# RWKV's state over eight chunks: three combined steps on the engines instead of six single ones

## The chip, the cores and the metric

The kernel runs on one core of a Trainium2 chip. Its time is the device time of one execution in microseconds, the median of the runs shown. The core's engines that compute are TensorE (PE; its weight loads are PEld), VectorE (DVE), ScalarE (ACT) and GpSimd (POOL); SyncE (SP) issues transfers. Each engine runs its own instruction stream in order and waits on semaphores for the others.

## The reference

A decoder trunk of two layers on a sequence of 512 positions, width 2048. Per layer one input projection, four mixers (RWKV-7, mLSTM, latent attention, differential attention), a gate, and one output projection:

```python
for l in range(DEPTH):
    h = rms_norm(x, norm_g[l])
    p = h @ w_in[l]
    z, p_rw, p_ml, p_mla, p_da = _split(p, IN_WIDTHS)
    y = concat([beta[0]*rwkv7(p_rw), beta[1]*mlstm(p_ml), beta[2]*mla(p_mla), beta[3]*diff_attn(p_da)])
    x = x + (y * silu(z)) @ w_out[l]
```

The change is in RWKV's recurrence, 8 heads of 64 x 64 state:

```python
def step(S, inp):
    r_t, w_t, k_t, v_t, kk_t, a_t = inp
    sa = einsum('bhvk,bhk->bhv', S, -kk_t)
    S = S * w_t[:, :, None, :] + sa[..., None] * (kk_t * a_t)[:, :, None, :] + v_t[..., None] * k_t[:, :, None, :]
    return S, einsum('bhvk,bhk->bhv', S, r_t)
```

Both kernels cut the 512 positions into `NCH` = 8 chunks of 64. Within a chunk everything is matrix products; between chunks the state obeys S[c+1] = G[c] S[c] + H[c], where G[c] is a 64 x 64 factor and H[c] a 64 x 64 term of the chunk alone.

## The kernel before, in words

**The projection fills everything.** The input projection is 16 groups of columns (`PIECES`, in the order in which the mixers need them), each of 16 steps (one 128-row slice of the weights) of 4 tiles. A tile is three matmuls of 128 x 512 (high x high, low x high, high x low part of the split float32 operands; L793 in `project`). A tile is named (step, tile) below; step n belongs to group n // 16, and tile m of every group accumulates in bank m of the four PSUM banks `ps_proj`. TensorE's program is one stream: the small products of a mixer, and between them `fill(name, head, j)`, which issues the next few tiles of the projection. How many tiles each name gets is the table `FILL` (L100 to 109); `planned` (L238) deals the list of tiles out to the names in program order. Names like `to_z_da` take all tiles up to the end of a group.

**What ScalarE does for the projection.** ScalarE walks the same plan. Where a fill holds the last step of a group (step 16g + 15), ScalarE's `fill` calls `evacuate(g, m)` (L1244): it waits until TensorE has finished that tile, and copies bank m to the staging buffer. ScalarE does nothing else meanwhile, and what stands behind the call in its own program waits with it. TensorE waits for the copy of bank m before it begins tile m of the next group (`s_proj_copied` in `project`):

```python
if k == 0 and g:
    in_bank = g - 1 if m < tiles_of(g - 1) else g - 2
    pe.wait_ge(s_proj_copied, tiles_before(in_bank) + m + 1)
```

So between the last tile m of a group and the first tile m of the next there are three other tiles, and the copy has to be through in that time.

**RWKV.** Two heads go together (a head pair, `hp` 0 to 3; head 0 in partitions 0 to 63 and head 1 in 64 to 127), four pairs per layer, eight in all. Per pair, in this order: fills `rw_lora` and `rw_factors`, the transposes (L989 to L992), `rw_turned`, the Gram products (L1002), the inversion by levels, then `rw_local`: after the products that give G and H of all chunks (L1098, L1101, L1104, 16 matmuls each), ScalarE copies H to `rw_st` (L1528), VectorE adds G's diagonal to give `rw_gt` (L1935, L1939). Then the state: for chunk 1 to 6, two matmuls (one for each head, L1114), a fill of one tile (`rw_state`), and on VectorE two linked additions (L1948), for which TensorE waits before the next chunk. `rw_state_last` is 0 tiles; L1120 and L1125 follow (the bonus sum, and the products of the states with the queries). A float32 matmul of this size shows as two records of the trace, so L1114's two matmuls are four.

**After RWKV** comes mLSTM, four heads. TensorE's order per head: fill `ml_qk`, wait for VectorE's q and k, the scores (L1154), fill `ml_s`, L1162, fill `ml_h`, L1169, L1171, fills `ml_gate` and `ml_rest`. ScalarE's order per head h around the places that matter:

```python
tanh_z(8 + h, ml_z, ml_e)          # L1273: waits until the stores of y have landed
fill("ml_qk", h)                   # ... exps of ml_w (L1590), fill ml_s, two squares ...
fill("ml_gate", h)
load_ln(); act.wait_ge(s_ml_h_var, h + 1)   # a table load; then Ln, Exp (L1605, L1606)
gate_of_convolution(h + 1)         # L1568
fill("ml_rest", h)
keep_y(8 + h, 4 + h, ml_yo, ml_z, ml_e)     # L1281 cast, waits for DVE L1710, stores (L1283, L1284)
```

With `ml_first=25, ml_qk=(19, 6, 13, 13), ml_s=8, ml_h=3, ml_gate=(0, 0, 9, 0), ml_rest=(22, 15, 6, 12)`. In `keep_y`, VectorE's `low_half` (L1710) waits for ScalarE's cast, and VectorE's L1994, which TensorE's scores wait for, stands behind L1710 in VectorE's program.

Where the plan of before puts the last tiles of the groups behind the first changed fill (the same in both layers): (143, 0..3) in `rw_lora` of pair 2, places 1 to 4 (counted from 0); (159, 0..3) in `rw_local` of pair 2, places 2 and 3, and in its first two `rw_state`; (175, 0..3) in `rw_turned` of pair 3, places 1 to 4 of 5; (191, 0..3) in `ml_first`, places 16 to 19; (207, 0..2) in `ml_qk` of head 1, places 3 to 5 of 6, and (207, 3) in `ml_s` of head 1; (223, 0..3) in `ml_rest` of head 2, places 2 to 5 of 6; (239, 0..3) at the end of `to_z_da`, which has 28 tiles.

Of the kernel before, what the change touches and what calls it, by code (L numbers as in the profile page):

```python
# [24 lines left out]
ACT = mybir.ActivationFunctionType  # L25
AX = mybir.AxisListType.X

P = 128
D, T, DEPTH = 2048, 512, 2
NT = T // P  # L30
# [6 lines left out]
NCH = T // RW_CHUNK  # L37
LEVELS = (2, 4, 8, 16, 32)
MASKED = -1e30
# [51 lines left out]
def tiles_of(g):  # L91
# [13 lines left out]
    rw_pu=(2, 2, 2, 2), rw_local=(4, 4, 4, 4), rw_outer=(1, 1, 1, 1), rw_state=(1, 1, 1, 1), rw_state_last=(0, 0, 0, 0),  # L105
# [132 lines left out]
def planned(counts):  # L238
# [27 lines left out]
    for h in range(4):  # L266
        for name in ("rw_lora", "rw_factors", "rw_turned"):
            place(name, h)
        for name in ("rw_gram", "rw_x"):
            place(name, h)  # L270
        for j in range(len(LEVELS)):
            place("rw_level", h, j)
            if j < len(LEVELS) - 1:
                place("rw_step", h, j)
        for name in ("rw_levels", "rw_pu", "rw_outer", "rw_local"):
            place(name, h)
        for j in range(1, NCH - 1):
            place("rw_state", h, j)
        for name in ("rw_state_last", "rw_carried"):
            place(name, h)  # L280
        if h == 0:
            place("to_z_rw", through=G_Z_RW)
        place("rw_gate", h)
# [40 lines left out]
def build(nc, a, out):  # L324

    with ExitStack() as ctx:
# [105 lines left out]
        rw_wl = rg(NCH)  # L432
# [258 lines left out]
        for layer in range(DEPTH + 1):  # L691
# [10 lines left out]
            with nc.Block() as block:  # L702
# [63 lines left out]
                def _(pe):  # L766
# [61 lines left out]
                    def fill(name, h=0, j=0):  # L828
                        for n, m in plan[name, h, j]:
                            (project if n < STEPS else out_early)(n, m)  # L830
# [143 lines left out]
                    for hp in range(4):  # L974
# [121 lines left out]
                        for i in range(NT):  # L1096
                            for c, q, h, half in quarters:
                                mm(ps[half, c, i * P:i * P + 64], rw_pu[q, 4 * h + i, 0:64], rw_bnT[q, i, half],  # L1098
                                   start=True, stop=True)
                            for c, q, h, half in quarters:  # L1100
                                mm(ps[half, c, i * P + 64:(i + 1) * P], rw_ktT[q, i, half], rw_vT[q, i, half],  # L1101
                                   start=True, stop=False)
                            for c, q, h, half in quarters:
                                last = mm(ps[half, c, i * P + 64:(i + 1) * P], rw_bnT[q, i, half],  # L1104
                                          rw_pu[q, 4 * h + i, 64:P], start=False, stop=True)
# [3 lines left out]
                        for c in range(1, NCH - 1):  # L1109
                            if c > 1:  # L1110
                                pe.wait_ge(s_rw_state_ready, (NCH - 2) * hp + c - 1)
                            for h in range(2):
                                half = slice(64 * h, 64 * h + 64)
                                last = mm(ps[half, h, c * 64:(c + 1) * 64], rw_gt[half, c, :], rw_st[half, c, :],  # L1114
                                          start=True, stop=True)
                            last.then_inc(s_rw_state_mm, 1)
                            fill("rw_state", hp, c)
                        fill("rw_state_last", hp)
                        pe.wait_ge(s_rw_state_ready, (NCH - 2) * (hp + 1))
# [103 lines left out]
                def _(act):  # L1223
# [245 lines left out]
                    for hp in range(4):  # L1469
# [57 lines left out]
                        for q in range(2):  # L1527
                            nc.scalar.activation(rw_st[:, 1 + q:NCH + 1:2, :], ps[:, q, :].rearrange("p (i s c) -> p i s c", i=NT, s=2)[:, :, 1, :], ACT.Copy).then_inc(s_rw_h_copied, 1)  # L1528
                        fill("rw_local", hp)
                        for c in range(1, NCH - 1):  # L1530
                            fill("rw_state", hp, c)
# [147 lines left out]
                def _(dve):  # L1679
# [180 lines left out]
                    for hp in range(4):  # L1860
# [70 lines left out]
                        v.tensor_copy(rw_pu[:, 4:8, :], ps[:, 1, :].rearrange("p (i c) -> p i c", i=NT)).then_inc(s_rw_pu_ready, 1)  # L1931
                        dve.wait_ge(s_rw_local, hp + 1)
# [5 lines left out]
                        for q in range(2):  # L1938
                            ins = v.tensor_tensor(rw_gt[:, q:NCH:2, :], rw_wli[:, q:NCH:2, :], ps[:, q, :].rearrange("p (i s c) -> p i s c", i=NT, s=2)[:, :, 0, :], ADD)  # L1939
                            if q:  # L1940
                                ins.then_inc(s_rw_local_ready, 1)
                            else:
                                link(ins)
                        for c in range(1, NCH - 1):
                            dve.wait_ge(s_rw_state_mm, (NCH - 2) * hp + c)
                            for h in range(2):
                                half = slice(64 * h, 64 * h + 64)
                                ins = v.tensor_tensor(rw_st[half, c + 1, :], rw_st[half, c + 1, :], ps[half, h, c * 64:(c + 1) * 64], ADD)  # L1948
                                if h:
                                    ins.then_inc(s_rw_state_ready, 1)  # L1950
                                else:
                                    link(ins)
# [153 lines left out]
```

## Time and profile before

| | |
|---|---|
| median of 3 runs | 2305.7 us (2302.61 to 2306.72) |
| the profiled execution | 2304.52 us, its span 2302.7 us |
| granted TensorE clock, mean | 0.999 |
| TensorE matmul busy | 2266.4 us, 98% of the span |
| GpSimd busy | 1744.8 us, 76% |
| VectorE, ScalarE busy | 1070.6 us (46%), 662.4 us (29%) |

The span is the time from the first to the last instruction in the profile. Busy of TensorE is the union of its matmuls, which overlap one another, so that one matmul's duration is longer than its share of time: the distance from start to start is what it costs in a row. In a timeline, a line is: start, duration, engine, line, operation, output and inputs, shape, count; in brackets the idle time of the engine ahead of it and what ended it.

### The profile page before, as it was taken

The numbers are of one execution on the slowest core, as the hardware profiler recorded it, in microseconds if no ns is written. First come the engines' busy times: TensorE is split into PE (matmuls) and PEld (weight loads), VectorE is DVE, ScalarE is ACT, GpSimd is POOL, SyncE is SP. The second block draws the span as 40 slices with busy tenths as digits, with TensorE's granted clock in tenths as the row PEclk, the third lists the DMA queues.
The fourth block names the chain that finished last, engine by engine and source line by source line (L and its number), as shares of the span: only waits on it lengthen the run. The fifth ranks groups of instructions, "written<-read, shape, count | busy, mean of one in ns | idle before, by whom it ended". The sixth has DMA issues, their size and how long they took to land. (4 is left out here: it accounts for less than half of the span.)

```text
span 2302.7 us, 38356 instructions
## 1 busy us (share of the span) xinstructions
PE 2266.4 (98%) x16032; PEld 1734.8 (75%) x16032; DVE 1070.6 (46%) x1411; ACT 662.4 (29%) x1193; POOL 1744.8 (76%) x1228
## 2 busy tenths in 40 slices
PE   7999999999999999999999999999999999999999
PEld 5767777777777778777777677767777777787777
DVE  5023327456363772465250232475474647625542
ACT  5222222222221332343341232223132213324421
POOL 3677679678587999988637766886685789998884
PEclk9999999999999999999999999999999999999999
DMA  4622343333234545732536232533332345456334
GB/s 161 192 85 78 103 146 116 91 100 99 84 109 134 160 149 173 254 95 77 149 106 175 82 101 82 165 89 97 93 114 83 95 147 165 138 198 230 89 83 128
DMA packets 165487, 288.64 MB, mean 125 GB/s; under 512 B 28792, under 2 KB 36344, under 8 KB 163776
## 3 DMA queue, kind: packets, MB, share of 16 engines
q1 hardware_dynamic: 125216, 211.60, 31.4%
q10 hardware_dynamic: 40096, 74.57, 9.8%
q8 instruction: 126, 2.06, 0.4%
q14 instruction: 49, 0.40, 0.1%
HBM read 234.43 MB, written 51.68 MB: 124 GB/s over the span
## 5 line engine op out<-in xcount | busy, mean ns | idle before, releaser
L752 POOL TENSOR_SCALAR w_hi<-raw 128x512 fp32r<-128x512 f32 x552 | 905.5, 1640 | 359.0 <-PE ps_proj L793 313.6
L762 POOL TENSOR_TENSOR w_lo<-raw,w_hi 128x512 fp32r<-128x512 f32 (+1 forms) x640 | 844.8, 1321 | 151.7 <-ACT w_hi L1251 96.3
L793 PE MATMUL ps_proj<-h_hi,w_hi 128*128 128x512 f32 (+1 forms) x1760 | 726.4, 413 | 6.2 <-POOL w_lo L762 3.5
L793 PE MATMUL ps_proj<-h_lo,w_hi 128*128 128x512 f32 (+1 forms) x1760 | 688.6, 391 | 0.0
L793 PE MATMUL ps_proj<-h_hi,w_lo 128*128 128x512 f32 x1728 | 675.6, 391 | 0.0
L793 PEld LDWEIGHTS ps_proj<-h_hi,w_hi 128*128 128x128 f32 (+1 forms) x1760 | 329.5, 187 | 107.7 <-issue 26.7
L793 PEld LDWEIGHTS ps_proj<-h_lo,w_hi 128*128 128x128 f32 (+1 forms) x1760 | 329.4, 187 | 73.6 <-DVE h_lo L1773 0.2
L793 PEld LDWEIGHTS ps_proj<-h_hi,w_lo 128*128 128x128 f32 x1728 | 325.7, 188 | 66.1 <-issue 7.7
L808 PE MATMUL ps_proj<-w_hi,h_hi 128*128 128x512 f32 x448 | 181.3, 405 | 0.4 <-POOL w_lo L762 0.4
L808 PE MATMUL ps_proj<-w_lo,h_hi 128*128 128x512 f32 x448 | 174.8, 390 | 0.0
L808 PE MATMUL ps_proj<-w_hi,h_lo 128*128 128x512 f32 x448 | 174.8, 390 | 0.0
L793 PE MATMUL ps_proj<-w_hi,h_hi 128*128 128x512 f32 x256 | 105.1, 411 | 0.0
L808 PEld LDWEIGHTS ps_proj<-w_hi,h_hi 128*128 128x128 f32 x448 | 84.2, 188 | 26.0 <-issue 8.5
L1792 DVE TENSOR_REDUCE arena<-ps 128x1 f32<-128x128 f32 (+3 forms) x96 | 47.1, 491 | 121.4 <-PE ps L1205 63.7
L1244 ACT ACTIVATE stage<-ps_proj 128x512 f32<-128x512 f32 (+1 forms) x118 | 66.5, 601 | 124.8 <-PE ps_proj L793 121.5
L793 PE MATMUL ps_proj<-w_hi,h_lo 128*128 128x512 f32 x256 | 99.9, 390 | 0.0
L793 PE MATMUL ps_proj<-w_lo,h_hi 128*128 128x512 f32 x256 | 99.9, 390 | 0.0
L808 PEld LDWEIGHTS ps_proj<-w_lo,h_hi 128*128 128x128 f32 x448 | 84.2, 188 | 18.1 <-issue 1.9
L808 PEld LDWEIGHTS ps_proj<-w_hi,h_lo 128*128 128x128 f32 x448 | 84.1, 188 | 18.0
L1251 ACT ACTIVATE w_hi<-raw 128x512 fp32r<-128x512 f32 (+1 forms) x88 | 48.9, 561 | 148.1 <-PE ps_proj L793 76.5
L1657 ACT ACTIVATE arena<-ps,arena 128x128 f32<-128x128 f32 (+3 forms) x64 | 38.7, 616 | 109.8 <-DVE arena L1793 109.8
L1718 DVE TENSOR_TENSOR arena<-arena,ps_proj 128x512 f32<-128x512 f32 x48 | 31.2, 680 | 68.1 <-PE ps_proj L808 68.1
(349 smaller groups left out, 2953.6 us busy)
## 6 DMA issues: line engine op xcount, KB each, us to landing
raw<-in_w_in_dram SPq DMA_DIRECT2D x480, 256.0 KB, 2.7
raw<-in_w_out_dram SPq DMA_DIRECT2D x128, 256.0 KB, 3.1
projected<-stage SPq DMA_DIRECT2D x116, 256.0 KB, 2.8
arena<-projected ACTq DMA_DIRECT2D x90, 256.0 KB, 3.1
out_dram<-arena ACTq DMA_DIRECT2D x7, 1024.0 KB, 4.8
gated_hi<-arena ACTq DMA_DIRECT2D x24, 256.0 KB, 2.6
gated_lo<-arena ACTq DMA_DIRECT2D x24, 256.0 KB, 3.2
h_hi<-gated_hi SPq DMA_DIRECT2D x8, 768.0 KB, 5.8
```

The costliest lines, as they stand in the source:

```text
L752: nc.gpsimd.tensor_scalar(hi, src, 1.0, None, ALU.mult).then_inc(s_hi_split, 1)
L762: nc.gpsimd.tensor_tensor(lo, src, hi.bitcast(F32), ALU.subtract).then_inc(s_raw_split, 1)
L793: last = mm(ps_proj[rows, m, :], lhsT, rhs, start=(k == 0 and j == 0), stop=(k == KT - 1 and j == len(products) - 1))
L808: last = mm(bank[:, i, :], lhsT, rhs, start=(first and j == 0), stop=(last_k and j == 2))
L1244: nc.scalar.activation(stage[0:rows, m, :], ps_proj[0:rows, m, :], ACT.Copy).then_inc(s_proj_copied, 1)
L1251: nc.scalar.activation(w_hi[:, at_all % N_SPLIT, 0:width], raw[:, at_all % N_RAW, 0:width], ACT.Copy).then_inc(s_hi_by_act, 1)
L1657: nc.scalar.activation((da_p_first, da_p)[half][:, b, 0:(i + 1) * P], ps[:, b, 0:(i + 1) * P], ACT.Exp, scale=da_rq[:, 4 * half + b:4 * ha ...
L1718: v.tensor_tensor(part, part, bank[:, i, :], ADD).then_inc(s_out_added, 1)
L1792: link(v.tensor_reduce(mx[:, b:b + 1], ps[:, b, 0:(i + 1) * P], AX, MAX))
```

## The change

`STATE_STEPS` = 3 replaces the six steps. In step 0 TensorE forms the products of state for chunks 1, 4 and 6, and beside them products of neighbouring chunks' factors (G3 with G4, transposed and not, and G5 with G6). In step 1, states for chunks 2 and 5 and the pair 5-6, and two longer products of factors. In step 2, four products that all start at state 3 and give states 4 to 7. A step issues 12, 10 and 8 matmuls of 64 x 64 (two of before). VectorE adds the states, in steps 0 and 1 copies the products of factors with the halves exchanged (4 instructions each), and in step 2 does one addition. In the local part, G of chunk 7 (not used) goes, copies of G3 and G5 in the other orientation are formed in its place (4 matmuls for 2), and chunk 7's H is left out (4 matmuls fewer). VectorE gets one small copy and does three additions for two. ScalarE's second copy of H has three tiles for four. In `FILL`, `rw_local` goes from 4 to 5 tiles and `rw_state` from 1 to 2 tiles a step, so a head pair takes 5 + 3 x 2 = 11 tiles there, before 4 + 6 x 1 = 10.

(Common indentation is left out in each part.)

```diff
--- before.py
+++ after.py
@@ -36,6 +36,7 @@
 NCH = T // RW_CHUNK
 LEVELS = (2, 4, 8, 16, 32)
+STATE_STEPS = 3
 MASKED = -1e30
 
 
@@ -102,7 +103,7 @@
 la_probs=(13, 13, 13, 13), la_turned=(3, 3, 3, 3), la_gate=(4, 4, 4, 4),
 rw_first=8, rw_lora=(13, 11, 11, 11), rw_factors=(26, 28, 28, 28), rw_turned=(5, 5, 5, 5),
 rw_gram=(4, 4, 4, 4), rw_x=(2, 2, 2, 2), rw_level=(1, 1, 1, 1), rw_step=(1, 1, 1, 1), rw_levels=(1, 1, 1, 1),
-rw_pu=(2, 2, 2, 2), rw_local=(4, 4, 4, 4), rw_outer=(1, 1, 1, 1), rw_state=(1, 1, 1, 1), rw_state_last=(0, 0, 0, 0),
+rw_pu=(2, 2, 2, 2), rw_local=(5, 5, 5, 5), rw_outer=(1, 1, 1, 1), rw_state=(2, 2, 2, 2), rw_state_last=(0, 0, 0, 0),
 rw_carried=(3, 3, 3, 3), rw_gate=(13, 14, 13, 12),
 ml_first=25, ml_qk=(19, 6, 13, 13), ml_s=(8, 8, 8, 8), ml_h=(3, 3, 3, 3), ml_gate=(0, 0, 9, 0), ml_rest=(22, 15, 6, 12),
 da_first=20, da_sums=(14, 10, 10, 10), da_scores=(7, 7, 7, 7), da_half=(14, 16, 16, 16), da_turned=(3, 3, 3, 3),
@@ -274,7 +275,7 @@
         place("rw_step", h, j)
 for name in ("rw_levels", "rw_pu", "rw_outer", "rw_local"):
     place(name, h)
-for j in range(1, NCH - 1):
+for j in range(STATE_STEPS):
     place("rw_state", h, j)
 for name in ("rw_state_last", "rw_carried"):
     place(name, h)
@@ -1095,28 +1096,48 @@
 fill("rw_outer", hp)
 for i in range(NT):
     for c, q, h, half in quarters:
-        mm(ps[half, c, i * P:i * P + 64], rw_pu[q, 4 * h + i, 0:64], rw_bnT[q, i, half],
-           start=True, stop=True)
-    for c, q, h, half in quarters:
+        if 2 * i + c == NCH - 1:
+            mm(ps[half, 1, 3 * P + 64:4 * P], rw_bnT[q, 1, half], rw_pu[q, 4 * h + 1, 0:64], start=True, stop=True)
+            mm(ps[half, 1, 3 * P:3 * P + 64], rw_bnT[q, 2, half], rw_pu[q, 4 * h + 2, 0:64], start=True, stop=True)
+        else:
+            mm(ps[half, c, i * P:i * P + 64], rw_pu[q, 4 * h + i, 0:64], rw_bnT[q, i, half],
+               start=True, stop=True)
+    used = quarters if i < NT - 1 else quarters[:2]
+    for c, q, h, half in used:
         mm(ps[half, c, i * P + 64:(i + 1) * P], rw_ktT[q, i, half], rw_vT[q, i, half],
            start=True, stop=False)
-    for c, q, h, half in quarters:
+    for c, q, h, half in used:
         last = mm(ps[half, c, i * P + 64:(i + 1) * P], rw_bnT[q, i, half],
                   rw_pu[q, 4 * h + i, 64:P], start=False, stop=True)
 last.then_inc(s_rw_local, 1)
 fill("rw_local", hp)
 pe.wait_ge(s_rw_local_ready, hp + 1)
-for c in range(1, NCH - 1):
-    if c > 1:
-        pe.wait_ge(s_rw_state_ready, (NCH - 2) * hp + c - 1)
-    for h in range(2):
-        half = slice(64 * h, 64 * h + 64)
-        last = mm(ps[half, h, c * 64:(c + 1) * 64], rw_gt[half, c, :], rw_st[half, c, :],
-                  start=True, stop=True)
+three, five = rw_gt[:, 0, :], rw_gt[:, NCH - 1, :]
+g_t = [rw_gt[:, c, :] for c in range(NCH - 1)]
+k_34, k_34_turned, k_56, k_345, k_3456 = (rw_wli[:, j, :] for j in range(5))
+state_products = (
+    ((g_t[1], 1), (g_t[4], 4), (g_t[6], 6)),
+    ((g_t[2], 2), (g_t[5], 5), (k_56, 5)),
+    ((g_t[3], 3), (k_34, 3), (k_345, 3), (k_3456, 3)))
+chunk_products = (
+    ((three, g_t[4]), (g_t[4], three), (five, g_t[6])),
+    ((k_34_turned, g_t[5]), (k_34_turned, k_56)),
+    ())
+for step in range(STATE_STEPS):
+    if step:
+        pe.wait_ge(s_rw_state_ready, STATE_STEPS * hp + step)
+    for j, (factor, c) in enumerate(state_products[step]):
+        for half in halves:
+            last = mm(ps[half, 0, j * 64:(j + 1) * 64], factor[half, :], rw_st[half, c, :],
+                      start=True, stop=True)
+        if j < len(chunk_products[step]):
+            lhsT, rhs = chunk_products[step][j]
+            for q, o in swapped:
+                last = mm(ps[o, 1, j * 64:(j + 1) * 64], lhsT[q, :], rhs[q, :], start=True, stop=True)
     last.then_inc(s_rw_state_mm, 1)
-    fill("rw_state", hp, c)
+    fill("rw_state", hp, step)
 fill("rw_state_last", hp)
-pe.wait_ge(s_rw_state_ready, (NCH - 2) * (hp + 1))
+pe.wait_ge(s_rw_state_ready, STATE_STEPS * (hp + 1))
 mm(ps[:, 0, :], bones, rw_sq, start=True, stop=True).then_inc(s_rw_bonus_sum, 1)
 for c in range(1, NCH):
     fed = slice(256 + c // 2 * 64, 256 + c // 2 * 64 + 64)
@@ -1525,10 +1546,10 @@
 act.wait_ge(s_rw_local, hp + 1)
 
 for q in range(2):
-    nc.scalar.activation(rw_st[:, 1 + q:NCH + 1:2, :], ps[:, q, :].rearrange("p (i s c) -> p i s c", i=NT, s=2)[:, :, 1, :], ACT.Copy).then_inc(s_rw_h_copied, 1)
+    nc.scalar.activation(rw_st[:, 1 + q:NCH:2, :], ps[:, q, :].rearrange("p (i s c) -> p i s c", i=NT, s=2)[:, 0:NT - q, 1, :], ACT.Copy).then_inc(s_rw_h_copied, 1)
 fill("rw_local", hp)
-for c in range(1, NCH - 1):
-    fill("rw_state", hp, c)
+for step in range(STATE_STEPS):
+    fill("rw_state", hp, step)
 fill("rw_state_last", hp)
 act.wait_ge(s_rw_carried, hp + 1)
 nc.scalar.activation(rw_kk.rearrange("p (i c t) -> p c i t", i=NT, c=2), y_parts, ACT.Square).then_inc(s_rw_y_squared, 1)
@@ -1929,27 +1950,30 @@
 v.tensor_tensor(xt, xt, ps[:, 2:4, 0:256], SUB).then_inc(s_rw_xt_stepped, 1)
 dve.wait_ge(s_rw_pu_mm, hp + 1)
 v.tensor_copy(rw_pu[:, 4:8, :], ps[:, 1, :].rearrange("p (i c) -> p i c", i=NT)).then_inc(s_rw_pu_ready, 1)
+link(v.tensor_copy(rw_wl[:, 0:NCH:NCH - 1], rw_wl[:, 3:7:2]))
 dve.wait_ge(s_rw_local, hp + 1)
 chunks_ar = rw_ar[:, :, 1, :].rearrange("p i (c t) -> p c i t", c=2)
 link(v.tensor_tensor(chunks_ar, chunks_ar, ps[:, 2:4, 0:256].rearrange("p c (i t) -> p c i t", i=NT), ADD))
 link(v.tensor_tensor(rw_wli, eye64[:, None, :].to_broadcast([P, NCH, 64]), last_w, MUL))
 
 dve.wait_ge(s_rw_h_copied, 2 * hp + 2)
-for q in range(2):
-    ins = v.tensor_tensor(rw_gt[:, q:NCH:2, :], rw_wli[:, q:NCH:2, :], ps[:, q, :].rearrange("p (i s c) -> p i s c", i=NT, s=2)[:, :, 0, :], ADD)
-    if q:
-        ins.then_inc(s_rw_local_ready, 1)
-    else:
-        link(ins)
-for c in range(1, NCH - 1):
-    dve.wait_ge(s_rw_state_mm, (NCH - 2) * hp + c)
-    for h in range(2):
-        half = slice(64 * h, 64 * h + 64)
-        ins = v.tensor_tensor(rw_st[half, c + 1, :], rw_st[half, c + 1, :], ps[half, h, c * 64:(c + 1) * 64], ADD)
-        if h:
-            ins.then_inc(s_rw_state_ready, 1)
-        else:
-            link(ins)
+link(v.tensor_tensor(rw_gt[:, 2:NCH:2, :], rw_wli[:, 2:NCH:2, :], ps[:, 0, P:].rearrange("p (i s c) -> p i s c", i=NT - 1, s=2)[:, :, 0, :], ADD))
+link(v.tensor_tensor(rw_gt[:, 0, :], rw_wli[:, 0, :], ps[:, 1, 3 * P + 64:4 * P], ADD))
+v.tensor_tensor(rw_gt[:, 1:NCH:2, :], rw_wli[:, 1:NCH:2, :], ps[:, 1, :].rearrange("p (i s c) -> p i s c", i=NT, s=2)[:, :, 0, :], ADD).then_inc(s_rw_local_ready, 1)
+products = ps[:, 0, 0:256].rearrange("p (j c) -> p j c", j=4)
+chunked = ps[:, 1, 0:192].rearrange("p (j c) -> p j c", j=3)
+dve.wait_ge(s_rw_state_mm, STATE_STEPS * hp + 1)
+link(v.tensor_tensor(rw_st[:, 2, :], rw_st[:, 2, :], products[:, 0, :], ADD))
+link(v.tensor_tensor(rw_st[:, 5:8:2, :], rw_st[:, 5:8:2, :], products[:, 1:3, :], ADD))
+link(v.tensor_copy(rw_wli[0:64, 0:3, :], chunked[64:P, :, :]))
+v.tensor_copy(rw_wli[64:P, 0:3, :], chunked[0:64, :, :]).then_inc(s_rw_state_ready, 1)
+dve.wait_ge(s_rw_state_mm, STATE_STEPS * hp + 2)
+link(v.tensor_tensor(rw_st[:, 3, :], rw_st[:, 3, :], products[:, 0, :], ADD))
+link(v.tensor_tensor(rw_st[:, 6:8, :], rw_st[:, 6:8, :], products[:, 1:3, :], ADD))
+link(v.tensor_copy(rw_wli[0:64, 3:5, :], chunked[64:P, 0:2, :]))
+v.tensor_copy(rw_wli[64:P, 3:5, :], chunked[0:64, 0:2, :]).then_inc(s_rw_state_ready, 1)
+dve.wait_ge(s_rw_state_mm, STATE_STEPS * hp + 3)
+v.tensor_tensor(rw_st[:, 4:8, :], rw_st[:, 4:8, :], products, ADD).then_inc(s_rw_state_ready, 1)
 dve.wait_ge(s_rw_bonus_sum, hp + 1)
 link(v.tensor_tensor(rw_bonus, ps[:, 0, :], vv, MUL))
 dve.wait_ge(s_rw_rstd, hp + 1)
```

## Rows read from the trace of the kernel before

**Rows 1.** The page, part 1: busy us (share of the span) and instructions, by engine.

```profile
PE 2266.4 (98%) x16032; PEld 1734.8 (75%) x16032; DVE 1070.6 (46%) x1411; ACT 662.4 (29%) x1193; POOL 1744.8 (76%) x1228
```

**Rows 2.** Timeline of layer 0, TensorE: start us, us, engine, line, operation [idle before].

```profile
230.62 0.47 PE L793 MATMUL ps_proj<-h_hi,w_hi 128*128 128x512 f32 x1 [0.53 <-ACT stage L1244]
```

**Rows 3.** Timeline, first head pair: local products and state, TensorE.

```profile
428.99 0.34 PE L1098 MATMUL ps<-arena 64*64 64x64 f32 x8
...
430.55 0.50 PE L793 MATMUL ps_proj<-h_hi,w_hi 128*128 128x512 f32 x1
...
433.49 0.33 PE L1114 MATMUL ps<-arena 64*64 64x64 f32 x4
...
434.64 0.20 PEld L1114 LDWEIGHTS ps<-arena 64*64 64x64 f32 x4 [0.36 <-DVE arena L1948]
...
440.35 1.02 PE L1120 MATMUL ps<-arena,always 128*128 128x512 f32 x2
```

**Rows 4.** The same stretch, VectorE.

```profile
425.09 0.69 DVE L1931 COPY arena<-ps 128x512 f32<-128x512 f32 x1 [1.27 <-PE ps L1075]
...
432.13 0.88 DVE L1939 TENSOR_TENSOR arena<-arena,ps 128x256 f32<-128x256 f32 x2
...
433.87 0.47 DVE L1948 TENSOR_TENSOR arena<-arena,ps 64x64 f32<-64x64 f32 x2 [0.86 <-PE ps L1114]
```

**Rows 5.** The same stretch, the products of states with queries.

```profile
441.30 0.89 PEld L1125 LDWEIGHTS ps<-arena 64*64 64x64 f32 x28 [0.76 <-issue]
```

**Rows 6.** Timeline, a wait of TensorE that VectorE ends.

```profile
401.95 1.40 DVE L1909 TENSOR_TENSOR arena<-ps,arena 128x512 f32<-128x512 f32 x2
...
403.41 0.27 PE L1020 MATMUL ps<-arena 64*64 64x64 f32 x1 [0.18 <-DVE arena L1909]
```

**Rows 7.** Timeline, layer 0, mLSTM head 0 to head 1, ScalarE, VectorE and TensorE.

```profile
781.56 0.64 ACT L1281 ACTIVATE arena<-arena 128x512 fp32r<-128x512 f32 x1 [2.96 <-DVE arena L1701]
...
785.65 1.09 DVE L1710 TENSOR_TENSOR arena<-arena 128x512 fp32r<-128x512 f32 x1
...
786.67 1.21 DVE L1994 SCALAR_TENSOR_TENSOR arena<-arena 128x1024 f32<-128x1024 f32 x1
786.78 0.33 ACTq L1283 DMA_DIRECT2D gated_hi<-arena  x1
...
789.32 0.39 PE L793 MATMUL ps_proj<-h_hi,w_hi 128*128 128x512 f32 x1
...
790.43 0.58 ACT L1244 ACTIVATE stage<-ps_proj 128x512 f32<-128x512 f32 x1
...
790.68 2.32 PE L1154 MATMUL ps<-arena 128*128 128x512 f32 x8
```

**Rows 8.** Timeline, layer 0, mLSTM head 2, ScalarE and TensorE.

```profile
836.90 1.28 ACT L1287 ACT_TABLE_LOAD   x1
...
840.09 0.64 ACT L1605 ACTIVATE arena<-arena 128x512 f32<-128x512 f32 x1 [1.70 <-DVE arena L2013]
...
842.58 1.04 ACT L1568 ACTIVATE arena<-arena 128x1024 f32<-128x1024 f32 x1
...
845.35 2.64 ACT L1244 ACTIVATE stage<-ps_proj 128x512 f32<-128x512 f32 x4 [1.72 <-PE ps_proj L793]
...
845.83 0.39 PE L793 MATMUL ps_proj<-h_hi,w_hi 128*128 128x512 f32 x1
```

**Rows 9.** Timeline, layer 0, pair 3, behind the transposes.

```profile
669.47 2.07 ACT L1244 ACTIVATE stage<-ps_proj 128x512 f32<-128x512 f32 x4
...
669.81 0.39 PE L793 MATMUL ps_proj<-h_hi,w_hi 128*128 128x512 f32 x1
```

**Rows 10.** Timeline, layer 1, pair 2, `rw_lora`.

```profile
1691.37 0.39 PE L793 MATMUL ps_proj<-h_hi,w_hi 128*128 128x512 f32 x1
...
1691.49 1.58 ACT L1244 ACTIVATE stage<-ps_proj 128x512 f32<-128x512 f32 x3 [0.72 <-PE ps_proj L793]
...
1692.23 0.47 PE L793 MATMUL ps_proj<-w_hi,h_hi 128*128 128x512 f32 x1
```

## The prediction

> **What bounds the kernel now.** The page's first part shows TensorE with a matmul in flight for 98% of the span, the next engine at 76% [rows 1]. So time goes down only by what TensorE stops doing between its matmuls, and it goes up by everything that makes TensorE wait. I then asked for the waits, longest in total first. No wait of TensorE's on VectorE in the six steps is over 0.4 us. One other kind is to be kept in mind: TensorE waits for ScalarE's copy of a finished bank, 0.53 us at one place [rows 2]. Last I read the timelines of the first state stage, and of each place where ScalarE copies banks behind it.
>
> In the state stage the reader is to see a period of 1.15 us from step to step (433.49 to 434.64), six of them 6.86 us in all [rows 3]. A tile of the projection costs 0.68 us (six matmuls in 1.36 us, 789.32 to 790.68 [rows 7]). The other 0.47 us are the four records and the change to the small matmuls and back. The view blames VectorE for 0.36 us, but VectorE was done at 433.87 + 0.47 = 434.34, 0.30 us before TensorE went on [rows 3, 4]; where VectorE really holds TensorE, the gap from its end (403.35) to the matmul is 0.06 us [rows 6]. So VectorE isn't what a step costs; the switch is.
>
> **The change, part by part, for one head pair.**
>
> *Three switches fewer.* The six tiles stay, so 3 x 0.47 = 1.41 us go.
>
> *More small products.* 60 records instead of 24, of which 12 are in the three switches that stay. With all four quadrants of the array in turn, 96 records took 1.56 us (428.99 to 430.55 [rows 3]), 0.016 us each; with two quadrants, 28 took 0.76 us (0.89, less a load's 0.13) from first to last start [rows 5], 0.028 each. Step 0 (24 records in four quadrants) costs 0.38 us, step 1 (16 and 4) 0.37, step 2 (16 in two) 0.45; less 3 x 0.11 for the twelve already counted it is +0.87 us. Net: -0.54 us.
>
> *The local products.* Four matmuls go, two come. But those for G3 and G5 stand two by two on the same quadrant, and their eight records go at the two-quadrant rate, or one after the other. I take +0.25 us; bounds 0 and +0.4 (eight records at 2 x 0.028, none hidden).
>
> *VectorE between steps.* With a gap of 0.03 us behind each, an addition from PSUM takes 0.22 us at 64 columns and 0.42 at 256, and a copy at 512 0.69 [rows 4]: about 0.15 us and 1.05 ns a column. The trace has no copy that crosses the halves on VectorE; I take the same price. Step 0's four instructions are 0.22 + 0.28 + 0.35 + 0.35, with three gaps: 1.29 us. VectorE begins 0.38 us after a step's first matmul at four records (433.49 to 433.87), so some 0.65 at 24, and ends at 1.94; with 0.06 TensorE may go on at 2.00. Its own work lasts 0.38 + 0.36 (the switch) + 2 x 0.68 = 2.10. It is covered, by 0.1 us; from there on each 0.1 us of the two copies costs a pair 0.2. Step 1 is 1.15 us of VectorE, with 0.24 to spare, step 2 0.42: covered. The third addition of G and the small copy ahead of it add 0.3 us; TensorE has one more tile (0.68) to cover that, and VectorE had 0.48 us to spare (432.13 + 0.88 against 433.49 [rows 3, 4]).
>
> So a pair gains 0.54 - 0.25 = 0.29 us, eight pairs 2.3 us. Bounds: 5 us gained, or 1 us lost if the copies are slow.
>
> *The plan moves.* A pair now takes 11 tiles in these fills, before 10. The total is the same (`to_z_da` gives up four), but every later tile comes earlier in program order: by 1 tile after pair 0, and by 4 from mLSTM on. With them move ScalarE's copies of the finished banks, against ScalarE's other work. TensorE must have the copy of tile m three tiles, 2.04 us, after it finished that tile. I go through each end of a group.
>
> (191) lands at places 12 to 15 of `ml_first`, (159) wholly in `rw_local`, (239) is again the end of its fill: ScalarE has nothing between the copies there. Nothing changes.
>
> (207): now tile 0 is the *last* place of `ml_rest` of head 0, tiles 1 to 3 are places 0 to 2 of `ml_qk` of head 1, and (208, 1) is place 4. Between them stand `keep_y` and `tanh_z`. `ml_rest` ends with the matmul that starts 13 before 789.32, 786.37, and ends at 786.76. ScalarE, idle since 778.6, waits for it, copies to 787.4 (0.58), and only then makes the cast that before began at 781.56: 787.35 to 788.0. VectorE's L1710 (before at 785.65) starts at 788.05; the stores are issued 1.13 us behind its start, at 789.2; and from there to ScalarE's next copy of a bank, through the landing of the stores and L1273, before took 790.43 - 786.78 = 3.65 us. So (207, 1) is copied from 792.8 to 793.4. TensorE wants to begin (208, 1) at 789.32. It goes on at about 793.5 (a copy's end to the matmul is 0.16 us in [rows 10]): **4.2 us lost** [rows 7]. L1994, before at 786.67 to 787.9, slips to 790.3, still ahead of the scores. The bounds: 3.8, if L1710 is 0.4 us shorter, and 5.1, if the stores land later.
>
> (223): tiles 0 and 1 are now places 7 and 8 of `ml_gate` of head 2, ahead of `load_ln`; tiles 2 and 3 are places 0 and 1 of `ml_rest`, and (224, 2) is place 4. Before, ScalarE waited 1.72 us for (223, 0) at 845.35; four tiles earlier it is 842.63, and (223, 1) is copied by 843.9. Only now come the table load and its activation (1.5 us, 836.90 and on), then L1605 at 845.4, and L1568 2.49 us behind it (840.09 to 842.58) at 847.9. The copy of (223, 2) follows at 848.9 and ends at 849.5. TensorE wants (224, 2) at 845.83, and begins it at 849.65: **3.8 us lost** [rows 8]. The scores of head 3 are later by the same, which leaves VectorE's chain to them, 5.3 us late, still in time.
>
> (175): tiles 2 and 3 are now places 0 and 1 of `rw_turned`, and (176, 2) is place 4, at 669.81. ScalarE's first copy behind its work on the transposes is 669.47 to 670.06, and it is now that of (175, 2): 0.4 us lost [rows 9].
>
> (143): tile 0 is now in `rw_gate`, 1 to 3 in `rw_lora`, places 0 to 2. In layer 1 ScalarE's first copy there is done at 1692.0, TensorE went on at 1692.23 and would want it at 1691.37: 0.9 us, of which 0.2 were there before [rows 10]. In layer 0, where pair 2 has one activation less, about 0.1.
>
> A word on ScalarE's table loads. The load in head 2's chain is 1.28 us [rows 8]. The Trainium skill, "ScalarE: Activation LUTs", section "Rules for kernel authors", budgets about 2.7 us for every switch to another set. By its price the chain of (223), with two switches in it, would be some 2.8 us longer per layer, and the kernel 5.6 us slower than by the row; the row is for this very load, so I stay with it and give the rule no chance of its own.
>
> **The sum.** Layer 0: 4.2 + 3.8 + 0.4 + 0.1 = 8.5; layer 1: 4.2 + 3.8 + 0.4 + 0.7 = 9.1. Lost 17.6, gained 2.3: +15.3 us. The profiled execution of before took 2304.5 us, 1.2 under the median of the runs shown; it comes to 2319.8, and the median to 2321. Nothing gives the loss back: TensorE is the last engine in every stage behind it.
>
> **The rivals.**
>
> *The copies are hidden; the steps decide.* For it: at (223) ScalarE had 1.72 us to spare, and no wait of this kind is over the 0.53 us of [rows 2] by much. It asks that ScalarE's copy isn't stuck behind `keep_y` and the table load, that is, that my places of the tiles are wrong. Against it: where they were, they explain the rows of before (three copies ahead of L1154 and one behind, four behind L1568). Then only the 2.3 us are gained: 2303. If the local products cost nothing more either, 2301.
>
> *Half of it.* Only one of the two long stalls appears, for instance because ScalarE's cast and L1710 run in another order than I read: 2321 less 2 x 4, 2313.
>
> *VectorE becomes the bound in the steps.* With crossing copies at twice the price a pair loses 0.70 - 0.10 = 0.60 us in step 0 and 0.56 - 0.24 = 0.32 in step 1; it decides from a copy of 0.40 us on, in place of 0.35. Alone, without my stalls: 8 x (0.92 - 0.29) = 5 us slower, 2311. With them 2328. This is the one by which the steps themselves make the kernel slower. Against it: no row shows an operation of VectorE on half the partitions that is dearer than by its columns (L1948).
>
> *The local products cost more than the steps save.* By 0.4 us a pair for the two quadrants instead of 0.25: 1 us more, within the range.
>
> **How the numbers follow.** The stalls as worked out, 0.72: 2321, its own range 2316 to 2326. Half of them 0.10: 2313. Copies hidden 0.13: 2303, of which half at 2301 or below. VectorE as bound 0.05, with or without the stalls. From 2309 to 2327 the time should be found 8 times in 10. A change of less than 0.2% (4.6 us, 2301.1 to 2310.3) can't be told from none: faster 0.06, same 0.10, slower 0.84.
>
> **What would show it.** Each step right: in the timeline of each pair, three groups of L1114's successor 2.1 us apart, and 0.3 to 0.6 us less from the first to the bonus sum. In the waits: TensorE at L793 for ScalarE's L1244, some 17 us in all, in pieces of 4.2 and 3.8 in both layers, in `ml_qk` of head 1 and `ml_rest` of head 2. In ScalarE's lines: L1281 of head 0 five to six us later against TensorE, right behind a copy. I am wrong if that wait stays near 1 us, and the prediction then fails in the places of the tiles; if the pieces are there and smaller, it fails in the chain from cast to landing.

## The result, and the profile after

The changed kernel takes 2323.9 us (median of 4 runs, 2323.4 to 2325.6), the kernel before on the same chip 2304.8 (2302.6 to 2306.7). The ratio is 1.0085, with a 95% interval of [1.0072, 1.0097]: 19 us slower. The forecast was 2321, by its own sum 15.3 us slower.

The profiled execution took 2323.97 us, its span is 2322.2, and the mean granted clock 0.995 (before: span 2302.7, 0.999). Part 1 of the page of the changed kernel, to be laid beside [rows 1]; the second line is the costliest group of its part 5 (busy, mean ns of one | idle before it, what ended most of it):

```profile
PE 2271.0 (98%) x16288; PEld 1742.8 (75%) x16288; DVE 1069.8 (46%) x1403; ACT 662.1 (29%) x1193; POOL 1742.1 (75%) x1228
...
L794 PE MATMUL ps_proj<-h_hi,w_hi 128*128 128x512 f32 (+1 forms) x1760 | 727.1, 413 | 21.2 <-ACT stage L1265 17.6
```

Of the 19.5 us between the two spans TensorE is busy for 4.6; the other 15 us are idle time, and it stands in front of the projection, ended by ScalarE's copies. (The change shifts the lines: L793 is L794 now, L1244 is L1265, L1114 is L1131 and L1136, L1281 is L1302, L1710 is L1731, L1605 is L1626.) The view of waits says so too (total us, how many, the longest). The changed kernel's line, where the kernel before has 2.2 us in 4 waits, the longest 0.6:

```profile
PE ps_proj L794 <- ACT stage L1265: 18.2, 11, 4.2
```

**The first head pair.** Timeline of the changed kernel, TensorE and VectorE (start, us, engine, line, operation, [idle before]), to be laid beside [rows 3, 4]:

```profile
427.69 0.34 PE L1103 MATMUL ps<-arena 64*64 64x64 f32 x8
...
429.23 0.50 PE L794 MATMUL ps_proj<-h_hi,w_hi 128*128 128x512 f32 x1
...
432.86 0.27 PE L1131 MATMUL ps<-arena 64*64 64x64 f32 x2
...
433.37 0.50 PE L794 MATMUL ps_proj<-h_hi,w_hi 128*128 128x512 f32 x1
433.50 0.22 DVE L1966 TENSOR_TENSOR arena<-arena,ps 128x64 f32<-128x64 f32 x1 [1.57 <-PE ps L1136]
...
434.08 0.36 DVE L1968 COPY arena<-ps 64x192 f32<-64x192 f32 x1
...
434.48 0.35 DVE L1969 COPY arena<-ps 64x192 f32<-64x192 f32 x1
...
434.96 0.28 PE L1131 MATMUL ps<-arena 64*64 64x64 f32 x2
...
437.05 0.68 PE L1131 MATMUL ps<-arena 64*64 64x64 f32 x16
...
439.16 1.02 PE L1141 MATMUL ps<-arena,always 128*128 128x512 f32 x2
```

The three steps start at 432.86, 434.96 and 437.05: 2.1 us apart, as forecast. From the first to the bonus sum are 6.30 us, before 6.86 [rows 3]: 0.56 less, 4.5 in eight pairs. The local products, without the state's, take 1.54 us (427.69 to 429.23), before 1.56: they cost nothing more. VectorE's two copies across the halves take 0.36 and 0.35 us; the forecast had 0.35.

**mLSTM, head 0 to head 1**, changed kernel, beside [rows 7]:

```profile
786.42 0.60 ACT L1265 ACTIVATE stage<-ps_proj 128x512 f32<-128x512 f32 x1 [8.21 <-PE ps_proj L794]
...
786.91 0.62 ACT L1302 ACTIVATE arena<-arena 128x512 fp32r<-128x512 f32 x1
...
787.57 1.05 DVE L1731 TENSOR_TENSOR arena<-arena 128x512 fp32r<-128x512 f32 x1 [2.23 <-ACT arena L1302]
...
788.71 0.39 PE L794 MATMUL ps_proj<-h_lo,w_hi 128*128 128x512 f32 x1
...
791.75 0.63 ACT L1294 ACTIVATE arena<-arena 128x512 f32<-128x512 f32 x1 [1.57 <-DMA gated_lo<-arena]
792.28 0.58 ACT L1265 ACTIVATE stage<-ps_proj 128x512 f32<-128x512 f32 x1
...
792.91 0.79 PE L794 MATMUL ps_proj<-h_hi,w_hi 128*128 128x512 f32 x1 [3.81 <-ACT stage L1265]
793.51 0.63 PE L794 MATMUL ps_proj<-h_hi,w_lo 128*128 128x512 f32 x1
...
795.64 3.94 PE L1175 MATMUL ps<-arena 128*128 128x512 f32 x8
```

Before, the cast on ScalarE (L1281) ran at 781.56, when VectorE had its operand ready. Now the copy of tile (207, 0) stands ahead of it, and that copy waits 8.21 us for TensorE. From there all goes in file: copy, cast, L1731, the stores, their landing (1.57 us of waiting), L1294, and only then the next copy of a bank. TensorE meanwhile has run through the four tiles whose banks were free, (207, 1) to (208, 0), and stands still from 789.1 to 792.91. And behind the wait it runs at half its rate: matmuls of 512 columns start 0.42 us apart instead of 0.23, and the eight of the scores take 3.94 us where they took 2.32 [rows 7].

**Head 2**, changed kernel, beside [rows 8]:

```profile
849.23 1.28 ACT L1265 ACTIVATE stage<-ps_proj 128x512 f32<-128x512 f32 x2 [5.74 <-PE ps_proj L794]
...
850.52 1.28 ACT L1308 ACT_TABLE_LOAD   x1
...
852.05 0.63 ACT L1626 ACTIVATE arena<-arena 128x512 f32<-128x512 f32 x1
852.20 0.39 PE L794 MATMUL ps_proj<-h_lo,w_hi 128*128 128x512 f32 x1
852.70 1.28 ACT L1627 ACT_TABLE_LOAD   x1
...
854.53 1.04 ACT L1589 ACTIVATE arena<-arena 128x1024 f32<-128x1024 f32 x1
...
855.48 1.06 ACT L1265 ACTIVATE stage<-ps_proj 128x512 f32<-128x512 f32 x2
856.11 0.50 PE L794 MATMUL ps_proj<-h_hi,w_hi 128*128 128x512 f32 x1 [3.52 <-ACT stage L1265]
```

Again two copies wait 5.74 us for TensorE in front of a table load, two activations and a second load, and the next two copies wait behind them. Layer 1 has the same two waits, of 4.23 and 3.52 us; the small ones are 0.15 us (pair 3, in both layers) and, in layer 1, 0.60 (pair 2).

The granted clock by windows of the changed kernel (window, its length, busy us and instructions by engine, granted clock, DMA share, GB/s): the stretch behind each wait of layer 0, then the whole of mLSTM:

```profile
792.90:799.30 6.40, 6.39 (x13) 4.12 (x14) 0.00 (x0) 2.37 (x6) 1.23 (x1) 0.53 0.94 304
856.90:860.30 3.40, 3.40 (x10) 2.61 (x9) 3.22 (x6) 0.63 (x1) 1.70 (x2) 0.51 0.96 297
...
743.24:931.40 188.16, 180.56 (x755) 141.06 (x754) 101.50 (x119) 51.09 (x80) 161.82 (x109) 0.97 0.49 154
```

The same stage of layer 0 in the kernel before:

```profile
743.63:922.09 178.46, 178.19 (x766) 140.69 (x766) 103.17 (x119) 51.32 (x80) 165.39 (x111) 1.00 0.52 162
```

So behind each long wait the chip grants the lower of TensorE's two levels, 1.2 in place of 2.4 GHz, for some microseconds. The stage is 9.7 us longer in layer 0, though it now holds four tiles less (2.72 us): 12.4 us are lost there, of which the two waits are 7.65 us from start to start (3.97 and 3.68). Most of the rest is the clock, as e4 shows (4.4 us); 0.3 us have no row.

### The profile page after: what moved, and what is told of

Read it like the earlier page. It is cut to its first block and busy times, and to the rows that moved or that the text cites. A ratio compares the mean times of both kernels' runs of the same rounds, so it can differ in the third digit from the quotient of the medians.

```text
span 2322.2 us, 38868 instructions
## 1 busy us (share of the span) xinstructions
PE 2271.0 (98%) x16288; PEld 1742.8 (75%) x16288; DVE 1069.8 (46%) x1403; ACT 662.1 (29%) x1193; POOL 1742.1 (75%) x1228
## 5 line engine op out<-in xcount | busy, mean ns | idle before, releaser
L794 PE MATMUL ps_proj<-h_hi,w_hi 128*128 128x512 f32 (+1 forms) x1760 | 727.1, 413 | 21.2 <-ACT stage L1265 17.6
L794 PE MATMUL ps_proj<-h_lo,w_hi 128*128 128x512 f32 (+1 forms) x1760 | 690.5, 392 | 0.0
L794 PE MATMUL ps_proj<-h_hi,w_lo 128*128 128x512 f32 x1728 | 678.0, 392 | 0.0
L794 PEld LDWEIGHTS ps_proj<-h_hi,w_hi 128*128 128x128 f32 (+1 forms) x1760 | 330.6, 188 | 125.1 <-issue 27.0
L794 PEld LDWEIGHTS ps_proj<-h_lo,w_hi 128*128 128x128 f32 (+1 forms) x1760 | 330.6, 188 | 74.1
L794 PEld LDWEIGHTS ps_proj<-h_hi,w_lo 128*128 128x128 f32 x1728 | 326.9, 189 | 67.3 <-issue 7.7
L1265 ACT ACTIVATE stage<-ps_proj 128x512 f32<-128x512 f32 (+1 forms) x118 | 66.9, 599 | 172.9 <-PE ps_proj L794 168.7
L794 PE MATMUL ps_proj<-w_hi,h_hi 128*128 128x512 f32 x256 | 104.8, 410 | 0.6 <-ACT stage L1265 0.6
L794 PE MATMUL ps_proj<-w_hi,h_lo 128*128 128x512 f32 x256 | 99.9, 390 | 0.0
L794 PE MATMUL ps_proj<-w_lo,h_hi 128*128 128x512 f32 x256 | 99.9, 390 | 0.0
L809 PEld LDWEIGHTS ps_proj<-w_lo,h_hi 128*128 128x128 f32 x448 | 84.2, 188 | 18.2 <-issue 1.9
```

What stands on the lines that cost most here:

```text
L794: last = mm(ps_proj[rows, m, :], lhsT, rhs, start=(k == 0 and j == 0), stop=(k == KT - 1 and j == len(products) - 1))
L809: last = mm(bank[:, i, :], lhsT, rhs, start=(first and j == 0), stop=(last_k and j == 2))
L1265: nc.scalar.activation(stage[0:rows, m, :], ps_proj[0:rows, m, :], ACT.Copy).then_inc(s_proj_copied, 1)
```

## The experiments

**e1: the change with the old plan.** One tile less in `rw_local`, so a pair again takes ten:

```
-    rw_pu=(2, 2, 2, 2), rw_local=(5, 5, 5, 5), ...
+    rw_pu=(2, 2, 2, 2), rw_local=(4, 4, 4, 4), ...
```

> The changed kernel with rw_local back from 5 tiles to 4: a head pair takes 4 + 3 x 2 = 10 tiles, as before, so every last tile of a group and every copy of ScalarE's stands where it stood before; the three steps stay. Theory A (the loss is the moved copies: 17.6 us of waits by the prediction, 16 us more by the waits of the changed kernel, and what the slower clock behind them costs; the steps gain 0.56 us a pair): L794 waits for ScalarE's copy 2 us in all, as before, the granted clock is back at 0.999, and the kernel takes 2304.8 - 8 x 0.56 = 2300.3 us, 0.2% faster than before. Theory B (the steps themselves, with 60 records in place of 24 and VectorE's four instructions, cost the time): it stays near 2324. A risk in both: VectorE's local work, 0.2 us longer, now has only the old four tiles to hide it, with 0.23 us to spare.

Measured: 2298.95 us (6 runs), ratio to before 0.9973 [0.9962, 0.9985], clock 0.999. Its line of waits is before's again:

```profile
PE ps_proj L794 <- ACT stage L1265: 2.2, 4, 0.6
```

The three steps alone make the kernel 6 us faster (by the ratio 6.2, its interval is 3.5 to 8.8); eight pairs of 0.56 us are 4.5 of it, and in the profiled executions TensorE waits 2.0 us less for GpSimd's `w_lo` (1.5 against 3.5), which no row explains. All of the loss, and more, is the tile. It is also the fastest version of the study, faster than both kernels.

**e2: the old six steps with the new plan**, the counterpart:

```
-    rw_pu=(2, 2, 2, 2), rw_local=(4, 4, 4, 4), ... rw_state=(1, 1, 1, 1)
+    rw_pu=(2, 2, 2, 2), rw_local=(5, 5, 5, 5), ... rw_state=(1, 1, 1, 1)
```

> The kernel before, six steps and all, with rw_local 5 tiles for 4: a pair takes 11 tiles, as in the changed kernel, and the last tiles of the groups stand where they stand there. Theory A: the same waits as in the changed kernel, pieces of about 4.0 and 3.7 us in both layers, the clock at half speed behind them, and 2304.8 + 19.1 + 8 x 0.56 = 2328 us. Theory B: the plan alone moves nothing, 2305.

Measured: 2328.2 us (4 runs), ratio 1.0095 [1.0080, 1.0111], clock 0.994, and the same waits without any new step in the kernel:

```profile
PE ps_proj L793 <- ACT stage L1244: 18.4, 11, 4.2
```

It is 4.3 us above the changed kernel by the medians and 2.3 by the two ratios, which have some 4 us of uncertainty; eight pairs of 0.56 us give 4.5. So the six steps with the new plan are no better than the three, and the waits come from the plan alone.

**e3: one of the two waits.** e1 with four more tiles in `ml_rest` of head 1, so that only the end of group 223 moves:

```
-    ... ml_rest=(22, 15, 6, 12),
+    ... ml_rest=(22, 19, 6, 12),
```

> The kernel of e1 with ml_rest of head 1 at 19 tiles for 15: the plan is shifted by four tiles from there on only, so (207) is as before and (223, 0) and (223, 1) are in ml_gate of head 2, ahead of the table load. Theory A: one wait of 3.5 to 3.7 us in each layer, 3.4 us at half clock behind it (1.7 us lost, as in the changed kernel), together 5.4 us a layer: e1 + 10.8 us, 2311. If the clock costs nothing: e1 + 7.2. Theory B: as e1.

Measured: 2311.7 us (10 runs), ratio 1.0024 [1.0015, 1.0033]; 12.8 us above e1, by the ratios 11.8. Waits, and the timeline at the wait in layer 0:

```profile
PE ps_proj L794 <- ACT stage L1265: 9.2, 6, 3.5
```

```profile
850.05 0.80 PE L794 MATMUL ps_proj<-h_hi,w_hi 128*128 128x512 f32 x1 [3.52 <-ACT stage L1265]
850.65 0.63 PE L794 MATMUL ps_proj<-h_hi,w_lo 128*128 128x512 f32 x1
...
855.34 0.63 PE L794 MATMUL ps_proj<-h_hi,w_hi 128*128 128x512 f32 x1
...
856.13 0.40 PE L794 MATMUL ps_proj<-h_lo,w_hi 128*128 128x512 f32 x1
```

The waits are 7.0 us more than e1's. Most of the other 5.8 is what the rows show behind them: here the half rate lasts from 850.65 to 855.77, twelve intervals of 0.43 us in place of 0.23, with the longer first one 2.7 us, and nearly as much in layer 1 (eleven such intervals). In the changed kernel the half rate behind this same wait lasts only 3.4 us, in both layers.

**e4: the long waits filled.** The changed kernel with 15 more matmuls of 512 columns, whose result is not read, ahead of the two tiles that wait:

```
+                            if (n, m) in ((13 * KT, 1), (14 * KT, 2)):
+                                for _ in range(15):
+                                    mm(ps[:, 3, :], h_hi[:, 0, 0:P], h_hi[:, 0, :], start=True, stop=True)
```

> The changed kernel with 15 matmuls of 128 x 512 more, whose result nobody reads, ahead of tiles (208, 1) and (224, 2) in each layer: TensorE computes for 3.4 us in the time in which it would wait. Theory A with the clock as a cost of its own: the wait for the copy shrinks to 0.3 to 0.6 us a piece, the granted clock stays at 0.999, and the kernel is faster than the changed one by what the half clock cost, 20.5 us at half speed or up to 10 us: 2314 to 2316. Theory C (the half clock costs nothing, its share of the loss is something else): 2324, as the changed kernel, since TensorE is kept as long as before.

Measured: 2317.6 us (4 runs), ratio 1.0049 [1.0036, 1.0063]. ScalarE's chain is as long as before, but the clock stays up (timeline, layer 0; lines are three further on):

```profile
789.49 3.56 PE L833 MATMUL ps<-h_hi 128*128 128x512 f32 x15
...
793.63 0.50 PE L794 MATMUL ps_proj<-h_hi,w_hi 128*128 128x512 f32 x1 [0.59 <-ACT stage L1268]
...
795.13 2.32 PE L1178 MATMUL ps<-arena 128*128 128x512 f32 x8
...
850.05 0.39 PE L794 MATMUL ps_proj<-h_lo,w_hi 128*128 128x512 f32 x1
...
853.96 0.50 PE L794 MATMUL ps_proj<-h_hi,w_hi 128*128 128x512 f32 x1
...
927.68 0.93 PE L1229 MATMUL ps<-arena 64*128 64x128 f32 x8
```

This prices the clock. From the end of the first wait to the last matmul ahead of the second, the same work takes 56.42 us (793.63 to 850.05) against 59.29 in the changed kernel (792.91 to 852.20): 2.87. From the second wait to the stage's end it takes 73.72 (853.96 to 927.68) against 75.29 (856.11 to 931.40, the same matmuls' start in the changed kernel): 1.57.

```profile
931.40 0.93 PE L1226 MATMUL ps<-arena 64*128 64x128 f32 x8
```

Together 4.44 us; layer 1 gives 2.91 and 1.60 by the same rows, 4.51. That is 8.9 in the kernel. The ratios say 1.0085 - 1.0049, 8.3 us, with some 4 us of uncertainty, and the two profiled spans differ by 6.7.

**e5: fewer tiles between the steps.** e1 with one tile behind each step in place of two, and three more ahead of the first:

```
-    ... rw_local=(4, 4, 4, 4), rw_outer=(1, 1, 1, 1), rw_state=(2, 2, 2, 2), ...
+    ... rw_local=(7, 7, 7, 7), rw_outer=(1, 1, 1, 1), rw_state=(1, 1, 1, 1), ...
```

> The kernel of e1 (three steps, 10 tiles a pair, every copy where it was) with rw_local 7 and rw_state 1 in place of 4 and 2: each step has one tile less to hide VectorE's four instructions. From the changed kernel's timeline VectorE ends 1.97 us after the first matmul of step 0 and 1.80 after that of step 1, and TensorE can go on 0.06 later; its own work with one tile is 2.10 - 0.68 = 1.42 and 1.41. So it would wait 0.6 us in step 0 and 0.45 in step 1, 1.05 us a pair, and in step 2 nothing: e1 + 8.4 us, 2307. That would show that the second tile is what hides VectorE, and that VectorE's price is real. The other theory, that steps cost TensorE only its switches, whatever the fill: e1 as it is, 2299.

Measured: 2307.5 us (10 runs), ratio 1.0011 [1.0002, 1.0020]; 8.5 us above e1. The waits that are new, 7.6 of the 8.5 us, and the matmuls that wait in the first pair:

```profile
PE ps L1131 <- DVE arena L1969: 4.4, 8, 0.6
PE ps L1131 <- DVE arena L1974: 3.2, 8, 0.4
```

```profile
435.10 0.14 PEld L1131 LDWEIGHTS ps<-arena 64*64 64x64 f32 x2 [0.99 <-DVE arena L1969]
435.10 0.28 PE L1131 MATMUL ps<-arena 64*64 64x64 f32 x2 [0.55 <-DVE arena L1969]
```

Now VectorE's chain is bare: step 0 lasts 2.02 us (433.08 to 435.10), where I had 2.00, and step 1 1.86. With two tiles it is 2.10, so the cover was indeed thin, 0.08 us, and it held. VectorE as the bound is refuted for the changed kernel; with one tile less behind each step it is the bound.

**e6 and e7: how far the plan may slip.** e1 with the fifth tile in the last two pairs only (mLSTM's tiles come two earlier, as against four in the changed kernel and none in e1), and in the last three (three earlier):

```
e6:  rw_local=(4, 4, 5, 5)
e7:  rw_local=(4, 5, 5, 5)
```

> The kernel of e1 with rw_local 5 in pairs 2 and 3 alone: the plan is shifted by two tiles behind RWKV instead of none or four. By the theory of the moved copies: (207, 0) is in place 1 of ml_qk of head 1, (208, 0) in place 5, 0.7 us ahead of the scores; ScalarE's copy behind its tanh is done at the time of 791.2 in the trace of before, TensorE wants the tile at 790.0: 1.2 us of wait a layer; (223) is wholly in ml_rest, behind L1568: none; (175, 0) is the first behind the transposes: 0.4 us. Together 3.2 us, no fall of the clock: 2302. If the loss simply went with the number of tiles moved: half of 20 us and more, 2309.

> The same with rw_local 5 in pairs 1 to 3: three tiles. By the theory of the moved copies (223, 0) is now the last place of ml_gate, ahead of the table load, and (224, 1) has to wait for (223, 1) as long as with four tiles: 3.7 us, with the half clock behind it; (208, 0) is in place 4 and waits 1.9 us, (143) and (175) 0.7 and 2 x 0.4: 12.7 us of waits and 3 to 7 of clock: 2316. In proportion to the tiles it would be 2314, so it is the waits that tell: a piece of 3.5 us that the kernel with two tiles has not.

Measured: e6 2303.0 us (11 runs), ratio 0.9994 [0.9985, 1.0002]; e7 2319.5 (4 runs), 1.0064 [1.0051, 1.0078]. The waits, first of e6, then of e7:

```profile
PE ps_proj L794 <- ACT stage L1265: 2.7, 6, 0.6
```

```profile
PE ps_proj L794 <- ACT stage L1265: 14.7, 11, 3.5
```

e7 came 3.5 us above its expected 2316. Its long waits are 2.15 and 2.30 us at head 0 and 3.52 at head 2 of each layer. Behind head 0's the rate stays full, behind head 2's it is halved, for 3.4 us in layer 0 (below) and for 2.9 us, from the first matmul on, in layer 1 (2001.88 to 2004.80, granted clock 0.50):

```profile
790.18 0.47 PE L794 MATMUL ps_proj<-h_hi,w_hi 128*128 128x512 f32 x1 [2.15 <-ACT stage L1265]
790.49 0.39 PE L794 MATMUL ps_proj<-h_hi,w_lo 128*128 128x512 f32 x1
...
851.38 0.63 PE L794 MATMUL ps_proj<-h_hi,w_hi 128*128 128x512 f32 x1
```

Of the 20.6 us above e1 the waits are 12.5 and the clock 3.1 (twice the 1.57 of e4), 1.5 more are waits for GpSimd's w_lo (3.0 us, in e1 1.5); the last 3.5 have no row. In e6 a wait of 1.2 us a layer was expected at (208, 0) and did not come. The reason is on VectorE (e6, layer 0): four operations of L2010 took 3.46 us, in the changed kernel 4.53, and L1731 0.69 where it took 1.05, so ScalarE's copy began at 787.67, in time. Layer 1 shows the same 3.46 and 0.69 us.

```profile
780.13 3.46 DVE L2010 SCALAR_TENSOR_TENSOR arena<-arena 128x512 f32<-128x512 f32 x4
...
783.51 0.69 DVE L1731 TENSOR_TENSOR arena<-arena 128x512 fp32r<-128x512 f32 x1
```

e6 is still 4.0 us above e1 (their spans 3.4) with only 0.5 us more of these waits. Part of the rest is TensorE's scores waiting for VectorE's L2018, 1.2 us in two waits where e1 has none; the remainder is scattered or unexplained. The loss is not in proportion to the slip: two tiles cost 4 us, three 20.6, four 25.0.

## Why the prediction was right, and what it missed

**The end of group 207: right.** Forecast 4.2 us a layer; the waits are 3.81 and 4.23, and from 788.71 to 792.91 the start-to-start time is 4.20 instead of 0.23, 3.97 lost. From L1731's start to ScalarE's copy I had 1.13 + 3.65 = 4.78 us, measured 4.71 (787.57 to 792.28). L2018 slipped and held nobody.

**The end of group 223: right.** Forecast 3.8, measured 3.52 of idle time, 3.68 start to start (852.20 to 856.11, less 0.23). The table loads are 1.28 us each, as in the row of before, and the activation behind a load starts 0.02 us after the load's end (851.80 and 851.82, behind the load at 850.52). (The Trainium skill, "ScalarE: Activation LUTs", "Rules for kernel authors", budgets about 2.7 us for every switch to a different set; this case's trace doesn't agree: a switch costs ScalarE 1.3 us here.)

**The small ones: right to 0.3 us.** (175) 0.15 for 0.4; (143) in layer 1 0.60 for 0.9.

All waits of this kind grew by 16.0 us (18.2 - 2.2); the forecast was 17.6. e2 shows that the plan alone makes them, e1 that the steps don't.

**The steps' gain: the mechanism right, the size too small.** Forecast 0.29 us a pair, measured 0.56 by the rows: 4.5 us in all, not 2.3 (e1's median says 6, with an interval that holds 4.5). The failed term is the +0.25 for the local products, which cost nothing (1.54 us against 1.56). Without it the sum is 0.54. The price of VectorE's copies (0.35) and the cover of 0.1 us stood (e5).

**The missing term: the clock.** "Nothing gives the loss back" was right, but nothing in the sum made it worse either, and something did: behind each long wait TensorE runs at about half its rate for 3.4 to 6.4 us. The rows of e4 put that at 8.9 us. With it the account closes: 16.0 + 8.9 - 4.5 = 20.4 us, against 19.5 between the two spans and 19.1 between the medians. Against the forecast of 17.6 - 2.3 = 15.3 that is 8.9 for the clock that was missing, less 1.6 of waits put too high and 2.2 of gain put too low. That the time came within 3 us of 2321 is in part luck: the last two errors hid 3.8 of the 8.9 us. Had those two terms been right, the sum with the clock would have been 2330, above the range that was given 8 chances in 10 (2309 to 2327).

**The rivals.** "Copies hidden" (2303) is what e1 is, and the changed kernel isn't. "Half of it" asked for one wait only; e3 made that case, and it costs 12.8 us above e1. VectorE as the bound: the crossing copies took 0.36 and 0.35 us, under the 0.40 from which it would decide, and e5 shows what happens when it does. "The local products cost more": they cost nothing. None was the case here.

## What to carry to other kernels

Where one engine's gaps are filled with work from a list dealt out by counts, one more piece at an early place moves all later ones; look up where each group then ends, and what the engine that must empty the banks has in its own order between those ends. Here the edit that was meant to cost nothing, one tile more per pair, cost 25 us, and the edit that was the point gained 6 us once the counts were set back. A long wait of TensorE is to be priced with what it does to the clock: here, behind waits of 3.5 to 4.2 us, it added over half of their own length (8.9 us to 15.1), and behind waits of 2.15 and 2.30 us nothing. What lies between was not measured.

## What the runs showed of the hardware that was not expected

- After idle stretches of 3.5 to 4.2 us TensorE was granted half its clock, not at once in every case: directly behind the wait at 792.91 and in e3 at 850.05, 0.8 us later in the changed kernel behind 856.11. It lasted 3.4 us there, 5.4 to 5.9 in e3, 6.4 behind 792.91, and in e7 3.4 in one layer and 2.9 in the other behind the same wait of 3.52 us; why it differs stays open. After idle stretches of 2.15 and 2.30 us (e7) the rate stayed full.
- VectorE's operations on SBUF alone vary from one version to another: L1731 took 0.69 us in e6 and 1.05 in the changed kernel, four of L2010 3.46 and 4.53, with nothing changed in them; L2018 behind them went the other way, 2.31 us in e6, 1.62 in the changed kernel and 1.21 in e1. It decided whether a wait of 1.2 us appeared. GpSimd was at work for 4.83 of the 5 us from 780 to 785 in e6 and in the changed kernel alike, so its load alone does not tell them apart; the cause was not isolated.
- 92 records of small matmuls over four quadrants took 1.54 us although eight of them stand two by two on the same quadrant: the rate of two quadrants, which the forecast used, did not show.
